# Ranking all eight experts of a mixture layer at its entry, with four instead of five taken at three passes

## The chip, the cores and the metric

The kernel is one program on one core of a Trainium2 chip. The metric is device time in microseconds for one execution. Five engines of the core share its on-chip memory (SBUF): TensorE (matmuls, into PSUM), VectorE, ScalarE, GpSimd and SyncE. Here SyncE only issues DMA. They synchronise by semaphores.

## The reference

Two decoder layers on 256 tokens of width 1024, in float32. Each has a mixer (gMLP beside latent attention) and a channel part; the second layer's channel part is a mixture of eight experts, two for each token. What matters here, cut short:

```python
logits = xt @ w_router + b_router                      # 256 tokens, 8 experts
top_val, top_idx = lax.top_k(logits, 2)
gates = softmax(top_val)
# every expert e, on the tokens that chose it:
hb = silu(xb @ w1[e]) * (xb @ w3[e])                   # 1024 -> 3584
yb = hb @ w2[e]                                        # 3584 -> 1024
out[token] += gate * yb
```

## The kernel before

**Products.** To keep float32 accuracy, each weight chunk `w` is split into `hi` (rounded, ScalarE, `moe_hi`, L744) and `lo = w - hi` (VectorE, `moe_lo`, L1289), activations likewise. A product is then three matmuls (`three`, L1987 to L1989): hi*hi, lo*hi and hi*lo. For an expert with at most 64 tokens the high and low parts of the activations stand side by side as 128 stationary columns, and two matmuls do (`two`, L2475 and L2476). Such an item is "small", with 64 slots; the others are "large", with 128.

**Items and units.** The expert stage runs eight items, one for each expert. An item is seven units (`NG`); a unit covers 512 of the 3584 hidden columns and loads six chunks of 1 MB: two each of w1, w3 and w2. There are 56 units and 336 loads, always the same. `LARGE = 5` says that items 0 to 4 are large; `SMALL_AT` says at which places of the sequence the small units stand: before, `LLLLLLLSLSLSLSLLSLSLSLSLLSLSLSLSLLSLSLSLSLLSLSLSLSLLSLLL`. Item 0 is always expert 0 and comes first; experts 1 to 7 are ranked by their counts (`expert_ranks`, `expert_order`, in the slots `TABLES` after units 0 and 1), so that the largest are items 1 to 4. An expert with more tokens than its item has slots gets a spare item of 42 more loads, at the end.

**Order.** Each engine's order is written out by hand in a function `unit(n)`. TensorE does w1 of unit n, turns the hidden rows of unit n-1 (L2515, L2512), w3 of unit n, then w2 of unit n-1. So the chunks come as w1, w3 of unit n, w2 of unit n-1, and the first load of unit n is number 6n-2 (loads count from 0). ScalarE copies or applies silu to the w1 result (L1087 small, L1089 large); this marks that w1 of a unit is done. VectorE makes the product with w3 (L1814, L1823) and the low part of the hidden rows (L1818, L1827).

**Weights.** SyncE issues the loads in order (`moe_load`, L533) into a ring of seven slots (five of `raw`, two in `r6`, shown as `r`). A slot is free when VectorE has taken the residual of its last content. The expert's number is read from SBUF by `value_load` (L550) when the unit's item starts.

**Tokens of an item.** For items after the first, VectorE picks the item's columns (`select`), TensorE and VectorE make row indices (`slot_rows`, `rows`), GpSimd gathers the rows by an indirect DMA (L695), TensorE turns them (L2461), ScalarE and VectorE split them. `PREP_AT` gives the four units in which this is done. Finished items are added to memory by indirect DMA from GpSimd (L705; a large item in one, a small one in two halves). Item 0's tokens are gathered by matmuls (`gather_first`, L2400) with one-hot columns made in `first_slots`, right after the router (`top_two`, `count`, L2395). `keep_busy` (L2056) issues matmuls whose result isn't used.

## Time and profile before

| | us |
|---|---|
| median of 3 runs | 1452.86 (1452.02 to 1453.07) |
| profiled execution, device time | 1452.38 |
| its span, first to last instruction | 1450.6 |
| first product of the expert stage | 555.84 |
| last matmul issued, end | 1438.4 |

The expert stage is thus about 880 of 1450 us. The page says how long each engine was busy; matmuls overlap each other, so that a busy TensorE isn't one at its fastest. "PEclk" is the granted clock in tenths of full speed. A line of a group ends with the idle time before its instructions and who ended it.

### The profile page before, as it was taken

Reading aid. Unit: us, or ns where it says so; the run is one execution under the profiler, and the core shown is the slowest. Engines: PE = TensorE matmul, PEld = TensorE weight load, DVE = VectorE, ACT = ScalarE, POOL = GpSimd, SP = SyncE. Lnnn points to the kernel's source line nnn. Section 1 sums busy time; section 2 is a strip of 40 time slices with the busy share of each in tenths; the row PEclk is TensorE's granted clock in tenths of the full one; section 3 lists DMA queues with packets and bytes.
Section 4 is the critical chain, followed back from the end, with each engine's and each line's share of the span. In section 5 each row is a group of like instructions: output and inputs, shape, how many; then the busy total and the mean of one; then the engine's idle time right before and its main releaser. Section 6 shows DMA issues by size and latency. Waiting matters only on the chain.

```text
span 1450.6 us, 19280 instructions
## 1 busy us (share of the span) xinstructions
PE 1423.5 (98%) x7352; PEld 1204.1 (83%) x7352; DVE 1279.9 (88%) x1263; ACT 1023.5 (71%) x992; POOL 75.3 (5%) x109
## 2 busy tenths in 40 slices
PE   9999999999999999999999999999999999999996
PEld 5799889878889988888888878888888778888884
DVE  6899888977777768999999999999999999999995
ACT  2764454444577358778887888888879888988874
POOL 5000000000000000000000001000000110000000
PEclk9999999999999999999999999999999999999999
DMA  9849849987553757999999999999999999999993
GB/s 373 330 176 349 327 174 386 391 336 277 184 198 140 285 200 277 382 414 360 407 422 421 420 416 407 410 421 420 422 421 408 414 416 420 419 408 421 418 384 129
DMA packets 74278, 506.91 MB, mean 349 GB/s; under 512 B 8386, under 2 KB 8514, under 8 KB 16707
## 3 DMA queue, kind: packets, MB, share of 16 engines
q1 hardware_dynamic: 69986, 490.91, 84.2%
q0 software_dynamic: 4192, 14.70, 3.3%
q8 instruction: 60, 0.98, 0.3%
q14 instruction: 40, 0.32, 0.1%
HBM read 498.74 MB, written 6.83 MB: 349 GB/s over the span
## 4 chain that ended last, share of the span: by engine, by line
PE 55%; issue 21%; DMA 10%; DVE 10%; ACT 3%; POOL 1%; SPq 0%; DVEq 0%; ACTq 0%; POOLq 0%
PE ps L1987 15%; PE ps L1989 14%; PE ps L1988 14%; DVE lo L1289 6%; DMA raw<-in_moe_w_dram 6%; DMA r<-in_moe_w_dram 3%; PE ps L2475 2%; PE ps L2476 2%; ACT hi L744 2%; PE ps L2048 2%; PE ps L2512 1%; DMA raw<-in_w_first_dram 1%; DMA gate_m<-rows_x,gather_row 1%; PE ps L2212 1%; PE ps L2195 1%
## 5 line engine op out<-in xcount | busy, mean ns | idle before, releaser
L1289 DVE TENSOR_TENSOR lo<-raw,hi 128x2048 fp32r<-128x2048 f32 x245 | 553.4, 2286 | 24.8 <-ACT hi L744 24.2
L744 ACT ACTIVATE hi<-raw 128x2048 fp32r<-128x2048 f32 x245 | 465.2, 1920 | 53.7 <-DMA raw<-in_moe_w_dram 44.0
L1987 PE MATMUL ps<-hi,hT_hi 128*128 128x512 f32 (+3 forms) x896 | 347.9, 388 | 4.0 <-DVE hT_lo L1315 1.9
L1989 PE MATMUL ps<-hi,hT_lo 128*128 128x512 f32 (+3 forms) x896 | 342.6, 382 | 0.0
L1988 PE MATMUL ps<-lo,hT_hi 128*128 128x512 f32 (+3 forms) x896 | 342.1, 382 | 0.0
L1289 DVE TENSOR_TENSOR lo<-r,hi 128x2048 fp32r<-128x2048 f32 x91 | 206.8, 2287 | 11.3 <-ACT hi L744 10.9
L1261 DVE TENSOR_TENSOR lo<-raw,hi 128x2048 fp32r<-128x2048 f32 (+3 forms) x83 | 177.0, 2145 | 37.7 <-ACT hi L728 29.6
L1987 PEld LDWEIGHTS ps<-hi,hT_hi 128*128 128x128 f32 x896 | 168.3, 188 | 38.9 <-issue 5.5
L1989 PEld LDWEIGHTS ps<-hi,hT_lo 128*128 128x128 f32 x896 | 168.2, 188 | 32.0
L1988 PEld LDWEIGHTS ps<-lo,hT_hi 128*128 128x128 f32 x896 | 168.4, 188 | 29.7
L744 ACT ACTIVATE hi<-r 128x2048 fp32r<-128x2048 f32 x91 | 173.4, 1921 | 19.6 <-DMA r<-in_moe_w_dram 15.5
L728 ACT ACTIVATE hi<-raw 128x2048 fp32r<-128x2048 f32 (+3 forms) x83 | 148.0, 1798 | 47.3 <-DMA raw<-in_w_fg_dram 26.2
L1987 PE MATMUL ps<-hi,bT_hi 128*128 128x512 f32 (+1 forms) x408 | 159.9, 392 | 4.2 <-DVE bT_lo L1818 4.0
L1989 PE MATMUL ps<-hi,bT_lo 128*128 128x512 f32 (+1 forms) x408 | 157.7, 386 | 0.0
L1988 PE MATMUL ps<-lo,bT_hi 128*128 128x512 f32 (+1 forms) x408 | 157.6, 386 | 0.0
L2475 PE MATMUL ps<-hi,bT_hi 128*128 128x512 f32 x392 | 154.3, 394 | 1.7 <-issue 1.0
L2476 PE MATMUL ps<-lo,bT_hi 128*128 128x512 f32 x392 | 152.8, 390 | 0.0
L1987 PEld LDWEIGHTS ps<-hi,bT_hi 128*128 128x128 f32 x408 | 76.6, 188 | 25.8 <-DVE bT_lo L1818 6.9
L1200 DVE SCALAR_TENSOR_TENSOR raw<-raw,c_rows 128x1024 f32<-128x1024 f32 x80 | 94.5, 1219 | 0.0
L1989 PEld LDWEIGHTS ps<-hi,bT_lo 128*128 128x128 f32 x408 | 76.6, 188 | 15.2
L2475 PEld LDWEIGHTS ps<-hi,bT_hi 128*128 128x128 f32 x392 | 73.6, 188 | 18.3 <-issue 1.5
L1988 PEld LDWEIGHTS ps<-lo,bT_hi 128*128 128x128 f32 x408 | 76.6, 188 | 14.3
(352 smaller groups left out, 1774.8 us busy)
## 6 DMA issues: line engine op xcount, KB each, us to landing
raw<-in_moe_w_dram SPq DMA_DIRECT2D x245, 1024.0 KB, 11.9
r<-in_moe_w_dram SPq DMA_DIRECT2D x91, 1024.0 KB, 12.1
raw<-in_w_ada_dram SPq DMA_DIRECT2D x40, 1024.0 KB, 6.8
raw<-in_w_fd_dram SPq DMA_DIRECT2D x11, 1024.0 KB, 6.9
raw<-in_w_ga_dram SPq DMA_DIRECT2D x8, 1024.0 KB, 6.4
raw<-in_w_gb_dram SPq DMA_DIRECT2D x8, 1024.0 KB, 5.4
raw<-in_w_ab_dram SPq DMA_DIRECT2D x8, 1024.0 KB, 4.8
raw<-in_w_o_dram SPq DMA_DIRECT2D x8, 1024.0 KB, 5.7
```

Of the source, the lines that this page charges most:

```text
L728: act.activation(high_of(s, e), raw_of(r, e), ACT.Copy).then_inc(hi_done, 1)
L744: act.activation(high_of(s), raw_of(r), ACT.Copy).then_inc(hi_done, 1)
L1200: m = dve.scalar_tensor_tensor(w, w, 1.0, cbc[:, :], ALU.mult, ALU.mult, accum_out=av[:, k:k + 1])
L1261: dve.tensor_tensor(low_of(s, e), raw_of(r, e), high_of(s, e).bitcast(f32), ALU.subtract).then_inc(raw_done, 1)
L1289: dve.tensor_tensor(low_of(s), raw_of(r), high_of(s).bitcast(f32), ALU.subtract).then_inc(raw_done, 1)
L1987: pe.matmul(o, wh, mh, start=first, stop=False)
L1988: pe.matmul(o, wh, ml, start=False, stop=False)
L1989: return pe.matmul(o, wl, mh, start=False, stop=last)
L2048: m = pe.matmul(ps[:, banks[t], 0:width], h0[:, k, t * P:(t + 1) * P], w[:, at:at + width], start=(k == 0), stop=(k == K - 1))
L2195: m = pe.matmul(ps[:, S_BANK[u], n * keys:(n + 1) * keys], qT[:, h, t * P:(t + 1) * P], kT[:, h, 0:keys], start=True, stop=True)
L2475: pe.matmul(o, both, mh, start=first, stop=False)
L2476: return pe.matmul(o, both, ml, start=False, stop=last)
```

## The change

`LARGE` becomes 4, and the sequence of units `LLLLSLSLSLSSLSLSLSSLSLSLSSLSLSLSSLSLSLSSLSLSLSSLSLSLSLLL`, with new places for the preparation of items. All eight experts are ranked by their counts before the stage: `expert_order` (with the ranking in it) follows the second `first_slots`, and the one-hot columns of item 0 are made behind it, in `item_slots`, from the ranked table. SyncE reads item 0's expert too, so that every load of the stage waits for `experts_ready`. ScalarE's `moe_hi(0, 1)` and `moe_hi(2)` and VectorE's `moe_lo(0, 1)` move from the routing to the first splits of item 0's tokens. The gates and their item tables are made once before unit 0. TensorE counts the totals right after the second tile's counts, and does ten and four `keep_busy` where it did one and two. `rows(0)` and `slot_rows(0)` move from unit 1 to unit 0.

```diff
-LARGE = 5
+LARGE = 4
-SMALL_AT = [7 + 9 * k // 4 for k in range((EXPERTS - LARGE) * NG)]
+SMALL_AT = [4 + (7 * k + 3) // 4 for k in range((EXPERTS - LARGE) * NG)]
-PREPS = (0, 5, 1, 2, 6, 3, 7, 4)
+PREPS = (0, 4, 1, 5, 2, 6, 7, 3)
-PREP_AT = {5: (2, 3, 4, 5), 1: (3, 4, 6, 7), 2: (14, 15, 16, 17), 6: (17, 18, 19, 20), 3: (25, 26, 28, 29),
-           7: (31, 32, 34, 35), 4: (39, 40, 42, 43)}
+PREP_AT = {4: (0, 1, 2, 3), 1: (6, 7, 9, 10), 5: (11, 12, 14, 15), 2: (19, 20, 22, 23), 6: (23, 24, 26, 27),
+           7: (35, 36, 38, 39), 3: (39, 40, 41, 42)}
@@ SyncE
-                if g == 0 and i:
+                if g == 0:
                     sp.wait_ge(experts_ready, 1)
                     expert[i] = sp.value_load(info[0:1, i:i + 1], min_val=0, max_val=EXPERTS - 1)
@@ ScalarE
             upto("m1.wo3")
-            moe_hi(0, 1)
...
             m.then_inc(xn_ready, 1)
-            moe_hi(2)
...
                 for b in (2 * h, 2 * h + 1):
                     first_high(b)
+                moe_hi(h)
+            moe_hi(2)
@@ VectorE
-            moe_lo(0, 1)
...
+            def expert_order():
+
+                dve.wait_ge(count_full, T + 1)
+                dve.tensor_copy(cnt, ps[:, R_BANK[1], 32:32 + E]).then_inc(ov_ready, 1)
+                dve.wait_ge(ov_ready, 1)
+                other = cnt.unsqueeze(1).to_broadcast([P, E, E])
+                own = cnt.unsqueeze(2).to_broadcast([P, E, E])
+                dve.tensor_tensor(cmp[:, 0], other, own, ALU.is_gt)
+                link(dve.tensor_tensor(eq[:, 0], other, own, ALU.is_equal))
+                link(dve.tensor_tensor(eq[:, 0], eq[:, 0], lt_mask[:, :, :], ALU.mult))
+                link(dve.tensor_tensor(cmp[:, 0], cmp[:, 0], eq[:, 0], ALU.add))
+                link(dve.reduce_sum(order, cmp[:, 0], AX))
+                link(dve.tensor_tensor(perm, order.unsqueeze(1).to_broadcast([P, E, E]),
+                                       eidx[:, :].unsqueeze(2).to_broadcast([P, E, E]), ALU.is_equal))
+                link(dve.tensor_tensor(ee, perm, eidx[:, :].unsqueeze(1).to_broadcast([P, E, E]), ALU.mult))
+                link(dve.reduce_sum(info_f[:, 0:E], ee, AX))
+                dve.tensor_copy(info[:, 0:E], info_f[:, 0:E]).then_inc(experts_ready, 1)
+                dve.wait_ge(experts_ready, 1)
...
             first_slots(1)
+            expert_order()
+            item_slots()
...
-                    first_low(h)
-                first_low(2)
-                first_low(3)
+                    first_low(2 * h)
+                    first_low(2 * h + 1)
+                    moe_lo(h)
                 moe_lo(2)
-                counted()
-                link(dve.tensor_copy(pg[:, :], slot_x[:, :, 0]))
+                gates()
+                item_gates()
+                picked(0, 0)
@@ TensorE
+            pe.wait_ge(sel_ready, 2)
+            count(0, 40, [(ones, 0), (before, 1)])
+            count(R_BANK[1], 32, [(ones, 0), (ones, 1)])
+            keep_busy(10, X_BANK[1])
             pe.wait_ge(hot0_ready, 1)
             gather_first(0, 0)
...
```

## Rows read from the trace of the kernel before

**Rows 1.** The page: busy time of the engines, and DMA in 40 slices.
```profile
PE 1423.5 (98%) x7352; PEld 1204.1 (83%) x7352; DVE 1279.9 (88%) x1263; ACT 1023.5 (71%) x992; POOL 75.3 (5%) x109
...
DMA  9849849987553757999999999999999999999993
```

**Rows 2.** Table by stretches: each engine's busy us, granted clock, DMA share, GB/s.
```profile
576.00:692.00 116.00, 115.41 (x535) 95.42 (x534) 110.27 (x112) 91.33 (x78) 4.90 (x3) 1.00 0.98 385
700.00:800.00 100.00, 99.95 (x474) 83.33 (x473) 97.19 (x60) 83.49 (x60) 0.00 (x0) 1.00 1.01 422
800.00:1350.00 550.00, 542.96 (x2568) 449.96 (x2567) 519.94 (x333) 467.15 (x372) 32.68 (x12) 1.00 1.01 416
```

**Rows 3.** Instructions in order of time, ScalarE: copies behind w1, units 2 and 3.
```profile
593.27 0.58 ACT L1089 ACTIVATE r<-ps 128x512 f32<-128x512 f32 x1
...
610.06 0.58 ACT L1089 ACTIVATE r<-ps 128x512 f32<-128x512 f32 x1
```

**Rows 4.** Instructions in order of time, TensorE: start, duration; first product, then pitch.
```profile
555.84 0.54 PE L1987 MATMUL ps<-hi,hT_hi 128*128 128x512 f32 x1
...
559.42 0.39 PE L1987 MATMUL ps<-hi,hT_hi 128*128 128x512 f32 x1
559.64 0.39 PE L1988 MATMUL ps<-lo,hT_hi 128*128 128x512 f32 x1
...
691.39 1.89 PE L2512 MATMUL ps<-r 128*128 128x64 f32 x16
```

**Rows 5.** Who waited for whom, 700 to 1400 us: total, times, longest.
```profile
ACT hi L744 <- DMA raw<-in_moe_w_dram: 41.1, 67, 2.0
```

**Rows 6.** Loads of line 533 from 700.2 to 1344.8 us: duration, first and last start.
```profile
L533 SPq DMA_DIRECT2D raw<-in_moe_w_dram x180: 332/333/337, 700.3 to 1344.7; - x180
...
L533 SPq DMA_DIRECT2D r<-in_moe_w_dram x72: 332/333/336, 705.2 to 1335.0; - x72
...
DMA to landing us min/median/max: 7.8/12.3/14.7
```

**Rows 7.** Three loads issued from 554.5 to 555.4 us into an empty queue.
```profile
DMA to landing us min/median/max: 4.8/8.4/10.4
```

**Rows 8.** Groups of instructions: busy us, mean ns, idle before and releaser.
```profile
L1289 DVE TENSOR_TENSOR lo<-raw,hi 128x2048 fp32r<-128x2048 f32 x245 | 553.4, 2286 | 24.8 <-ACT hi L744 24.2
L744 ACT ACTIVATE hi<-raw 128x2048 fp32r<-128x2048 f32 x245 | 465.2, 1920 | 53.7 <-DMA raw<-in_moe_w_dram 44.0
...
L1814 DVE TENSOR_TENSOR r<-r,ps 128x512 f32<-128x512 f32 x35 | 23.9, 682 | 1.9 <-PE ps L1989 1.6
```

**Rows 9.** Instructions in order of time, SyncE: first loads (merged; first start, time, count).
```profile
506.07 24.35 SPq L533 DMA_DIRECT2D raw<-in_moe_w_dram  x5
530.46 24.41 SPq L533 DMA_DIRECT2D r<-in_moe_w_dram  x2
```

**Rows 10.** Instructions in order of time: VectorE, second tile's slots, and two steps of the ranking.
```profile
552.17 0.17 DVE L1621 SCALAR_TENSOR_TENSOR r<-ps,r 128x8 f32<-128x8 f32 x1 [0.78 <-PE ps L2395]
...
570.50 0.22 DVE L1677 TENSOR_TENSOR r<-r 128x64 f32<-128x64 f32 x1
570.75 0.23 DVE L1678 TENSOR_TENSOR r<-r,lt_mask 128x64 f32<-128x64 f32 x1
```

**Rows 11.** Line 550, SyncE's reading of an expert's number: ns min/median/max.
```profile
L550 SPq TENSOR_LOAD <-info x7: 263/267/475, 644.3 to 1251.4; - x7
```

**Rows 12.** TensorE's wait for the first gather; all seven gathers' landing.
```profile
PE ps L2461 <- DMA gate_m<-rows_x,gather_row: 0.9, 1, 0.9
...
DMA to landing us min/median/max: 9.8/10.4/11.6
```

**Rows 13.** Load 311, issued at 1347.2, and the copy behind unit 52's w1.
```profile
DMA to landing us min/median/max: 12.1/12.1/12.1
...
1372.23 0.58 ACT L1087 ACTIVATE r<-ps 128x512 f32<-128x512 f32 x1
```

**Rows 14.** Table by stretches, the end of the program.
```profile
1440.00:1451.00 11.00, 0.00 (x0) 0.00 (x0) 4.50 (x8) 0.23 (x2) 0.00 (x0) 0.66 0.28 101
```

## What the change will do to the time: the prediction

> **What bounds the kernel now.** I read the page first, then a table by stretches, then who waits for whom, then single units. The page puts TensorE at 98%, VectorE at 88%, and the sixteen DMA engines at nearly 9 tenths from the 20th slice on [rows 1]. That leaves two candidates, so the expert stage is cut into stretches [rows 2]. From 576 to 692 us (seven units of item 0, all three passes) DMA brings 385 GB/s. From 700 to 800, with no indirect DMA, it brings 422; from 800 to 1350 it brings 416. The clock is 1.00, full speed, in all of them. The copies of ScalarE behind each w1 say what sets the first stretch: the large units 2 and 3 follow each other at 16.8 us [rows 3], more than six loads at the full rate need, for a load is 1.0486 MB, so 422 GB/s is 2.49 us a load, 14.9 us a unit.
>
> TensorE's own need per unit comes from its pitch: 0.23 us (559.42 to 559.64) from one 512-column matmul to the next, although each is shown as 0.39 long [rows 4]. Three passes are 72 of them, 16.4 us, plus the transposes, which with its waits is the 17 us seen. Two passes are 48, 10.9 us, and 16 short ones with 1.9: about 12.6. So the seven-unit opening is TensorE's, and after 700 the mean of TensorE (five of the one and four of the other, about 15.0) and DMA are within a few tenths. Who waits decides: from 700 to 1400 ScalarE waits 41.1 us, in 67 places, for weights to land in the five slots of `raw` alone [rows 5]. And 252 loads issued from 700.3 to 1344.7 took 12.3 us to land, against 4.8 for one issued into an empty queue [rows 6, 7]: about three others lie before each. A stream with a queue in front of it is what ends last. VectorE is close behind: six residuals of 2.29 us and two operations of 0.68 for the hidden part are 15.1 a large unit [rows 8]; they overlap by a few hundredths each, and the change leaves this as it is but for 0.5 us in seven units.
>
> The Trainium skill ("Perfetto Trace Analysis", Identifying the Most-Contended Engine) says that the busy share of TensorE doesn't tell how near it is to its limit. The trace agrees: 99.95 of 100 us are "busy" in a stretch where the pitch leaves room.
>
> **The change, part by part.**
>
> *Passes.* One item goes from three passes to two: seven units lose 24 matmuls each and gain twelve or so short ones, 17.0 - 12.6 = 4.4 us, 31 us of TensorE in all. The weights loaded remain 336. While DMA sets the pace this is worth nothing by itself. It shortens two things: how long the opening holds DMA below full rate (four three-pass units in a row instead of seven), and how far TensorE is behind the newest weights.
>
> *Does it fit?* I routed the reference's own inputs: the counts per expert are 18, 44, 16, 98, 107, 73, 31, 125. Ranked, the fifth has 44, under 64, and the first 125, under 128, so no spare item appears.
>
> *The head start is lost.* Item 0 was expert 0, so six of its loads were issued by 530.8 and three more at 554.5 to 555.4, before the routing was used [rows 9]. Now the first load waits for the ranking. The chain: the second tile's slots are computed at 552.17. The totals' count is one more pair of matmuls on two tiles, estimated at 0.4 like its neighbour, so the copy of counts starts at 552.6. Behind it come nine small operations of the ranking, which exist now too and follow each other at 0.25 us (570.50 to 570.75), the first two closer [rows 10]. So the cast ends at 554.9. SyncE reads the number in up to 0.48 us [rows 11]; with the address work behind it I take 0.9 to the issue (bounds 0.5 and 2): first load at **555.9**. Seven loads can then go at once, and the first lands after 4.9, at 560.8.
>
> *What the opening loses besides.* Copy and residual (1.92 + 2.29 [rows 8]) put TensorE's first product at about 565, against 555.84 now [rows 4]; the gathering matmuls that now follow the ranking end near 561, before that, so they cost nothing; with that cover gone they would cost a microsecond or two. The first w1 is done at 571, against 561.7. The gates and item tables (about 3.4 us of VectorE between residuals) move from the table slots of units 0 to 2 to ahead of unit 0's fourth residual; what is queued behind is every residual, and TensorE waits. That puts unit 1 at 585, unit 2 at 602, unit 3 at 619, at TensorE's 17 us. The stream's own line (560.8 + 2.49 for each load) is 573, 588 and 603 for these units' weights, so TensorE is 12 to 16 us behind a landing, where in the present opening the whole chain was over 20 behind and loads were held back.
>
> *Gather of the first small item.* Its rows are chosen in unit 1 and turned in unit 2. Now a gather lands 10.4 us after its issue, and TensorE waited 0.9 for the first [rows 12]. In the new place the index is ready near 594 and TensorE comes at 603, two or three microseconds before the rows. It costs TensorE that, in a stretch where it has less to give.
>
> *Early loss of the stream.* Put together, 0 (nothing held back) to 13 us (57 loads to unit 11 at the 385 GB/s pace of rows 2, 2.72 instead of 2.49 us). I take 1.5: the lag stays below the present opening's.
>
> *The stream.* The 252 loads of rows 6 are 251 intervals in 644.4 us, 2.567 each; at 2.49 they would be 625.0, so 19.4 us went to five gathers and seven scatters between them. Weighing a gather or a half scatter of 64 rows 1 and a whole accumulating scatter 2, that is 15 parts of 1.3 us. The new schedule has, before load 311, seven gathers, three whole and six half scatters: 19 parts, 24.7 us.
>
> *Sum.* Load 311 is the last that unit 52 needs for its gate product (the same number in both orders, and units 52 to 55 are small, large, large, large in both; 51 is large in both).
> 555.9 + 4.9 = 560.8; + 311 x 2.49 = 774.4, 1335.2; + 24.7 = 1359.9; the engines of a long queue don't end together (the third of three, issued 0.9 behind the first, lands after 10.4, where 4.8 + 2 x 2.49 - 0.9 would be 8.9 [rows 7]), 1.5 to 4, taken 2.5: 1362.4; + early loss 1.5: 1363.9. Now the load lands at 1347.2 + 12.1 = 1359.3 and its unit's copy is at 1372.23, 12.9 later [rows 13], where bare copy, residual and eight matmuls are 6.0: TensorE is behind. After the change it has 4 small in 7 units, 14.5 us a unit, against 15.4 of the stream; I take 10 (bounds 7 and 13). Copy of unit 52 at 1373.9, 1.7 later than now. The tail (three large units at TensorE's pace, drain, output) is unchanged, 78.4 us: span **1452.3**. Around the span lie 1452.38 - 1450.6 = 1.8, giving 1454.1; the profiled run is 0.5 below the median of the timed ones, so **1454.6**.
>
> **The rivals.**
>
> *A, the forecast, head start and shorter lag cancel:* 1450.5 to 1457.5. For it: every term is a row, and the sum lands 2 us from the present.
>
> *B, TensorE was the bound after all:* then 31 us less, plus the 9 us of the late start: about 1431. For it stands the 98% of the page; against it 422 GB/s with three loads queued.
>
> *C, the lag goes to its floor and nothing is lost early:* 7 instead of 10 and 0 instead of 1.5: 1450.1, at the edge of faster; with the 1.5 of spread, 1449.
>
> *D, slower: the opening fills the ring.* The place is units 1 to 10; the mechanism is late gates on VectorE, the early gather, and four 17 us units on top, so that loads wait for free slots. It decides from the point where a unit's first load is issued 29 us or more before its copy, as now in units 2 to 6. Price: half to all of the 13 us: 1459 to 1466, say 1462.
>
> *E, slower: TensorE's clock.* The granted clock reads 0.66 in the last stretch, after the last matmul at 1438.4, and 1.00 everywhere before, so here it fell to its half level only after a pause longer than any in the routing [rows 14]. The new opening has pauses of about 3 us (561.8 to 565, then between halves of w1), each broken by 1 to 3 us of matmuls. If it fell there, 7 us at half speed cost 3.5 in the opening, 1457.6. The Trainium skill ("TensorE: Matmul & The Clock Gate", HAM oscillation) warns against just this, products separated by waits for weights; no row of before shows a fall in such a pause.
>
> *F, it doesn't do what it says* (a spare item runs): 42 loads at 2.49, 105 us more, 1559. The counts exclude it but for a near tie.
>
> **How the numbers follow.** A 0.52, B 0.04, C 0.08, D 0.27, E 0.08, F 0.01. The forecast is A's 1454.6. Leaving out B, the far halves of C and D, and F leaves 1449.5 to 1462. A change of 0.2% (2.9 us) is about what can be told from none: the same means 1450.0 to 1455.8. Faster: B, most of C: 0.11. Slower: D, most of E, the upper end of A: 0.38. Same: 0.51.
>
> **What would show it.** First load near 555.9 and first product near 565; loads at 2.49 from there and 422 GB/s already before 692 (were it 385, D); copies of two-pass pairs within 13 us of a landing; the clock at 1.00 around 560 to 580; unit 52's copy near 1374 and 78.4 us behind it. Wrong would be the sum's first term if SyncE takes longer to read the expert, its third if the pace of loads depends on more than the queue, and the whole of it if the rate in the middle rises when TensorE has room, which is B.

## The result, and the profile after

| | before | after |
|---|---|---|
| median | 1452.44 us (4 runs, 1451.95 to 1453.07) | 1463.62 us (4 runs, 1461.62 to 1465.47) |
| profiled execution, device time | 1452.38 | 1465.47 |
| its span | 1450.6 | 1463.7 |
| copy behind w1 of units 0, 1, 2, 3 | 561.7, 575.9, 593.3, 610.1 | 575.8, 594.1, 611.3, 630.1 |
| of units 7, 14, 52 | 677.7, 782.5, 1372.2 | 689.7, 797.5, 1385.1 |

The changed kernel takes 1.0076 times as long, 95% interval 1.0059 to 1.0094, which is 11.2 us more. The forecast was 1454.6, with a range up to 1462.0. The page of the changed kernel (busy time; granted clock, DMA share and GB/s in 40 slices):

```profile
PE 1410.8 (96%) x7290; PEld 1193.4 (82%) x7290; DVE 1275.7 (87%) x1262; ACT 1026.3 (70%) x1006; POOL 80.3 (5%) x110
...
PEclk9999999999999998999999999999999999999998
DMA  9849849986544608999999999999999999999993
GB/s 374 325 178 346 331 174 393 379 353 243 200 173 166 252 30 343 376 376 422 417 398 421 421 409 420 421 421 407 409 421 421 420 422 408 408 420 420 416 389 129
```

TensorE is busy 12.7 us less than in [rows 1], and the time went up. (The split alone takes off 22.8, from the 1433.6 of the first experiment below; the new opening, with more fillers and a lower clock, puts 10 back. The prediction had 31 for the split.) The 16th slice (549 to 585 us) moves 343 GB/s, the 15th only 30: nothing runs ahead of the stage any more, and in the 16th the clock (PEclk) shows 8 tenths. The table by stretches, to be read beside [rows 2] (busy us of TensorE, its weight loads, VectorE, ScalarE, GpSimd; granted clock, DMA share, GB/s):

```profile
576.00:692.00 116.00, 112.79 (x522) 93.31 (x523) 107.15 (x96) 89.13 (x72) 2.30 (x1) 0.99 0.98 393
700.00:800.00 100.00, 96.72 (x468) 79.89 (x467) 97.02 (x66) 85.29 (x76) 6.33 (x2) 1.00 1.01 411
800.00:1350.00 550.00, 527.49 (x2508) 437.12 (x2507) 517.08 (x330) 469.45 (x376) 29.68 (x12) 0.99 1.01 417
554.00:560.00 6.00, 6.00 (x25) 5.02 (x25) 3.53 (x18) 0.22 (x1) 0.00 (x0) 0.72 0.46 158
566.00:572.00 6.00, 4.61 (x12) 3.31 (x12) 4.17 (x6) 4.14 (x4) 0.00 (x0) 0.72 1.01 427
```

The middle moves as much as before (417 against 416 GB/s) with 15 us less of TensorE in 550. The delay is largest at unit 3, 20.0 us; units 4 to 7 give 8.0 back, and from there to unit 52 it moves between 10 and 16, with no trend. The opening, in order of time. VectorE: the ranking's cast, then what it does until its second and third residual.

```profile
555.47 0.17 DVE L1637 CAST info<-r 128x8 int32<-128x8 f32 x1
...
561.15 0.73 DVE L1858 TENSOR_SCALAR r<-ps,scale_shift 128x128 f32<-128x128 f32 x2 [3.21 <-PE ps L2400]
...
564.89 2.29 DVE L1289 TENSOR_TENSOR lo<-raw,hi 128x2048 fp32r<-128x2048 f32 x1 [1.77 <-ACT hi L744]
...
570.42 4.49 DVE L1289 TENSOR_TENSOR lo<-raw,hi 128x2048 fp32r<-128x2048 f32 x2 [1.35 <-ACT hi L744]
```

TensorE in the same stretch: the count, ten fillers (each is shown as two records), the gathering products, the first product (it was at 555.84 [rows 4]).

```profile
552.16 0.39 PE L2395 MATMUL ps<-r,ones 128*128 128x8 f32 x2 [1.93 <-DVE r L1613]
...
553.08 6.25 PE L2056 MATMUL ps<-mask,ident 128*128 128x256 f32 x20
559.16 3.73 PE L2400 MATMUL ps<-r,x_tok 128*128 128x128 f32 x32
...
567.24 0.51 PE L1987 MATMUL ps<-hi,hT_hi 128*128 128x512 f32 x1 [2.62 <-DVE lo L1289]
```

The engines hand one chain to each other: ranking, gathering products (behind fillers that run partly at half clock), scaling, first copy, first residual. VectorE idles 3.2, 1.8 and 1.4 us in it. SyncE's first seven loads and their landing, where [rows 9] had the first at 506.07:

```profile
556.61 2.66 SPq L533 DMA_DIRECT2D raw<-in_moe_w_dram  x5
559.45 1.26 SPq L533 DMA_DIRECT2D r<-in_moe_w_dram  x2
```

```profile
DMA to landing us min/median/max: 6.3/12.3/17.9
```

Late in the stage: ScalarE's waits for weights from 700 to 1400 us (the row beside [rows 5]), the landing of load 311, issued at 1360.3, and unit 52's copy (beside [rows 13]):

```profile
ACT hi L744 <- DMA raw<-in_moe_w_dram: 36.6, 64, 2.5
```

```profile
DMA to landing us min/median/max: 11.5/11.5/11.5
```

```profile
1385.09 0.59 ACT L1085 ACTIVATE r<-ps 128x512 f32<-128x512 f32 x1
```

### The profile page after: what moved, and what is told of

Its sections match the earlier page's. It is cut to its first block, busy times and chain, and to the rows that moved or that the text cites. A ratio compares the mean times of both kernels' runs of the same rounds, so it can differ in the third digit from the quotient of the medians.

```text
span 1463.7 us, 19227 instructions
## 1 busy us (share of the span) xinstructions
PE 1410.8 (96%) x7290; PEld 1193.4 (82%) x7290; DVE 1275.7 (87%) x1262; ACT 1026.3 (70%) x1006; POOL 80.3 (5%) x110
## 4 chain that ended last, share of the span: by engine, by line
PE 68%; issue 15%; DVE 8%; DMA 5%; ACT 2%; POOL 0%; SPq 0%; DVEq 0%; ACTq 0%; POOLq 0%
PE ps L1987 16%; PE ps L1989 16%; PE ps L1988 16%; PE ps L2475 5%; PE ps L2476 5%; DVE lo L1289 4%; PE ps L2048 2%; DMA r<-in_moe_w_dram 2%; PE ps L2512 2%; DMA rows_y<-gate_m,scatter_row 1%; ACT hi L744 1%; PE ps L2212 1%; PE ps L2195 1%; DMA gate_m<-rows_x,gather_row 1%; DMA c_rows<-rows_x,gather_row 1%
## 5 line engine op out<-in xcount | busy, mean ns | idle before, releaser
L1289 DVE TENSOR_TENSOR lo<-raw,hi 128x2048 fp32r<-128x2048 f32 x245 | 553.2, 2287 | 26.7 <-ACT hi L744 26.1
L1987 PE MATMUL ps<-hi,hT_hi 128*128 128x512 f32 (+3 forms) x784 | 305.2, 389 | 7.5 <-DVE lo L1289 3.9
L1989 PE MATMUL ps<-hi,hT_lo 128*128 128x512 f32 (+3 forms) x784 | 300.1, 383 | 0.0
L1988 PE MATMUL ps<-lo,hT_hi 128*128 128x512 f32 (+3 forms) x784 | 299.9, 382 | 0.0
L1289 DVE TENSOR_TENSOR lo<-r,hi 128x2048 fp32r<-128x2048 f32 x91 | 206.8, 2287 | 7.9 <-ACT hi L744 7.7
L2475 PE MATMUL ps<-hi,bT_hi 128*128 128x512 f32 x448 | 178.6, 399 | 17.4 <-DVE bT_hi L1829 11.9
L2476 PE MATMUL ps<-lo,bT_hi 128*128 128x512 f32 x448 | 176.4, 394 | 0.0
L1987 PE MATMUL ps<-hi,bT_hi 128*128 128x512 f32 (+1 forms) x352 | 137.8, 392 | 4.5 <-DVE bT_lo L1820 4.5
L1989 PE MATMUL ps<-hi,bT_lo 128*128 128x512 f32 (+1 forms) x352 | 135.8, 386 | 0.0
L2475 PEld LDWEIGHTS ps<-hi,bT_hi 128*128 128x128 f32 x448 | 85.2, 190 | 38.8 <-DVE bT_hi L1829 14.0
L2475 PE MATMUL ps<-hi,bT_lo 128*128 128x512 f32 x224 | 89.1, 398 | 0.9 <-DVE lo L1289 0.8
L2476 PE MATMUL ps<-lo,bT_lo 128*128 128x512 f32 x224 | 87.5, 391 | 0.0
```

The source lines that it names most:

```text
L1289: dve.tensor_tensor(low_of(s), raw_of(r), high_of(s).bitcast(f32), ALU.subtract).then_inc(raw_done, 1)
L1987: pe.matmul(o, wh, mh, start=first, stop=False)
L1988: pe.matmul(o, wh, ml, start=False, stop=False)
L1989: return pe.matmul(o, wl, mh, start=False, stop=last)
L2475: pe.matmul(o, both, mh, start=first, stop=False)
L2476: return pe.matmul(o, both, ml, start=False, stop=last)
```

## The experiments

At the outset stands theory 1: the late opening is all of the loss, and removed passes pay only where TensorE sets the pace. Its rivals: a removed pass counts everywhere (2), the clock falls of the opening are the loss (3), or the serial order is, whatever the loads do (4). Ratios are to the kernel before, on the same chip, with their 95% interval. The experiments ran on several chips, on which the kernel before took 1452.0 to 1453.4 us, so a difference between two experiments is good to 1 us at best.

### Is it the opening or the split? Four combinations

**e1_entry_five**: the new opening, five large items in the old sequence.

```diff
-LARGE = 4
+LARGE = 5
-SMALL_AT = [4 + (7 * k + 3) // 4 for k in range((EXPERTS - LARGE) * NG)]
+SMALL_AT = [7 + 9 * k // 4 for k in range((EXPERTS - LARGE) * NG)]
...
```

> The opening of the changed kernel (first load waits for the ranking, all eight experts ranked at once) with the old split of the items: five of 128 slots with three passes, three of 64 slots, in the old sequence of units. Theory 1, the late opening is the whole loss and the removed passes pay only where TensorE sets the pace (units 4 to 7, where the delay shrank from 20 to 12 us): the 8 us that were given back are gone, 1463.6 + 8 = about 1471, and unit 14 comes 20 us later than before the change. Theory 2, the removed passes are worth their TensorE time everywhere (busy 20 us more with five large items): about 1484. If the split is worth nothing at all: 1463 to 1465.

Measured 1469.18 us, 1.0115 (1.0098 to 1.0132), near the 1471 of theory 1: unit 7 is 16.5 us late against 12.0 in the change. It is 1.8 less than expected, and the traces show why: here unit 3 came at 626.7, 16.6 late, and not 20.0. The changed kernel prepares its first small item in units 0 to 3, and its unit 3 lies 18.8 us behind unit 2, where this one has 16.8; of that TensorE waits 1.29 for the gather. So 3.4 of the 20.0 us come with the new split and not with the new opening, and the 8.0 that the split gives back are 4.5 net.

**e2_head_four**: four large items, with the first item's loads and first conversions where they had been.

```diff
-                if g == 0:
+                if i == 0 and g == 0:
+                    expert[0] = 7
+                elif g == 0:
                     sp.wait_ge(experts_ready, 1)
...
             upto("m1.wo3")
+            moe_hi(0, 1)
...
+            moe_hi(2)
...
-                moe_hi(h)
-            moe_hi(2)
...
+            moe_lo(0, 1)
...
-                    moe_lo(h)
```

> The new split (four and four) with the old head start: the first item's expert is written into the kernel as a constant (it is expert 7 for these inputs), so its loads and its first conversions stand where they stood before the change; all other items still wait for the ranking. Theory 1 (the loss is the head start): unit 0's copy is back at 562 to 565, the passes still return 8 us in units 4 to 7, and the time is 1452.4 - 8 = 1444, range 1443 to 1450. Theory 4 (the loss is the serial order of the ranking and selection work in the opening, whatever the loads do): 1458 to 1463. If transfers alone set the pace from the first load on: 1452.

Measured 1454.15 us, 1.0011 (1.0001 to 1.0020): neither the 1444 of theory 1 nor the 1458 of theory 4, and 2 us above the 1452 of a stream that alone sets the pace. The first copy came at 571.1, not 562 to 565.

**e3_loads_early**: as e2, but only the change on SyncE.

> The changed kernel with only the first item's loads early (its expert a constant); its conversions stay where the change put them, behind the ranking. If the loss is in the transfers (8 transfers less in the ring when the experts begin): the first copy may stay at 575, but the units behind it come 5 to 8 us earlier, 1456 to 1459. If the loss is the chain from the ranking to the first product (conversions, gather, one-hot, products at half clock): the first copy stays at 574 to 576, unit 1 at 592 to 594, and the time 1462 to 1464.

Measured 1464.07 us, 1.0086 (1.0069 to 1.0103), not to be told from the changed kernel, by the medians. Its four times spread over 6.5 us; in its profiled execution, the fastest of the four, the units came some 3 us earlier than in the change (unit 3 at 626.9), so a small gain of the early loads isn't excluded.

**e4_clock**: fillers in the pauses.

```diff
+            keep_busy(6, X_BANK[1])
             pe.wait_ge(sel_ready, 2)
...
-            keep_busy(4, X_BANK[1])
+            keep_busy(14, X_BANK[1])
```

> The changed kernel with 16 more filler products in the opening's pauses of TensorE (6 ahead of the count, 10 behind the gather), so that the clock does not fall to half at about 554, 568 and 578 us. Rival (the three falls of 3.4 us each at half clock are the loss, 1.7 us each): 1458 to 1459. Theory 1 (TensorE mostly waits for VectorE's and ScalarE's conversions there): 1462 to 1464, with the first copy less than 2 us earlier.

Measured 1462.38 us, 1.0065 (1.0048 to 1.0082). Two of the three falls are gone, and the third is hardly shorter (0.80, where the changed kernel has 0.73 from 578 to 584 us):

```profile
554.00:560.00 6.00, 6.00 (x43) 5.64 (x42) 3.82 (x18) 1.26 (x4) 0.00 (x0) 1.00 0.46 160
566.00:572.00 6.00, 4.82 (x22) 3.68 (x21) 4.43 (x4) 5.98 (x6) 0.00 (x0) 1.00 1.00 421
578.00:584.00 6.00, 6.00 (x23) 4.83 (x22) 3.09 (x4) 4.45 (x3) 0.00 (x0) 0.80 1.02 423
```

The first copy comes 2.0 us earlier, and the time is down by 1.2 us, within both intervals. Theory 3 falls as the main cause as far as the first two falls go; the third, some 3 us at half clock by the 0.73, was not removed.

**e8_old_opening_four**: the kernel before, with expert 7 pinned as item 0 and four large items, small units from unit 6.

```diff
-LARGE = 5
+LARGE = 4
-SMALL_AT = [7 + 9 * k // 4 for k in range((EXPERTS - LARGE) * NG)]
+SMALL_AT = [6 + (17 * k + 3) // 10 for k in range((EXPERTS - LARGE) * NG)]
...
-            expert = {0: 0}
+            expert = {0: 7}
...
```

> The kernel before with its opening as it was (first item known beforehand, its gather, one-hot and loads not behind the ranking) and four large items in place of five; expert 7, which is ranked first for these inputs, is the pinned one so that the items are those of the changed kernel, and the small units begin at unit 6 as their tables come no sooner. Theory 1 (the loss is the whole opening; the passes pay only where TensorE sets the pace): unit 0's copy at 561 to 563, 4 to 8 us ahead of the kernel before by unit 14, time 1452.5 - 4 to 8 = 1445 to 1449. Rival (four large items are worth nothing once the loads run ahead, as with the first conversions restored alone): 1452 to 1454.

Measured 1451.30 us, 0.9993 (0.9984 to 1.0003): no change that can be told.

| | five large | four large |
|---|---|---|
| old opening | 1452.3 (before) | 1451.3 (e8) |
| new opening | 1469.2 (e1) | 1463.6 (the change) |

Each against the kernel before on its own chip, the opening costs 12.2 us with four large items and 16.7 with five. The split returns 5.5 us with the new opening and 1.0 with the old one. So theory 1 has the place right, and misses something in the split: where the stage starts on time, four large items gained 1.0 us and not 4 to 8. One thing isn't held fixed in this table: in e8 the first small unit is unit 6, as its tables come no sooner, in the change it is unit 4. How much of 5.5 against 1.0 is due to that, no run separates.

What separates e3 from e2 is only that three copies and two residuals (some 10 us of ScalarE and VectorE) are done while the router waits. By the medians it is worth 9.9 us, all of the 9.5 from e2 to the change; in the two profiled executions it is 5.4. The table by stretches gives each engine's work up to 586 us, VectorE's being the third pair. The kernel before, then e8, e2, e3 and the change:

```profile
506.00:552.00 46.00, 45.35 (x283) 40.22 (x282) 28.99 (x51) 28.02 (x39) 3.98 (x6) 1.00 0.45 166
552.00:586.00 34.00, 33.67 (x166) 28.11 (x166) 30.94 (x48) 28.09 (x27) 0.00 (x0) 1.00 0.94 358
```

```profile
506.00:552.00 46.00, 45.44 (x283) 40.29 (x281) 29.58 (x51) 27.38 (x38) 3.77 (x6) 1.00 0.45 160
552.00:586.00 34.00, 33.58 (x166) 28.11 (x167) 30.31 (x49) 28.00 (x28) 0.21 (x1) 1.00 0.93 350
```

```profile
506.00:552.00 46.00, 44.95 (x280) 40.02 (x278) 29.30 (x46) 26.54 (x38) 2.93 (x3) 1.00 0.45 162
552.00:586.00 34.00, 32.49 (x162) 27.55 (x163) 26.48 (x64) 20.95 (x23) 1.08 (x4) 0.95 0.71 266
```

```profile
506.00:552.00 46.00, 44.76 (x279) 39.85 (x277) 24.89 (x45) 23.12 (x36) 3.13 (x3) 1.00 0.43 161
552.00:586.00 34.00, 27.93 (x135) 22.86 (x136) 25.52 (x63) 21.98 (x22) 0.89 (x4) 0.95 0.60 217
```

```profile
506.00:552.00 46.00, 43.94 (x272) 39.01 (x270) 24.77 (x48) 23.75 (x37) 3.94 (x6) 1.00 0.06 25
552.00:586.00 34.00, 28.68 (x125) 23.39 (x126) 21.95 (x55) 20.33 (x20) 0.07 (x1) 0.85 0.91 374
```

Up to 586 us VectorE has done 59.9, 59.9, 55.8, 50.4 and 46.7 us of work. Against e8 that is 0, 4.1, 9.5 and 13.2 us short for e8, e2, e3 and the change; the spans of these same executions are 0, 3.4, 8.8 and 13.4 us longer. Bytes don't order them: the change moved 374 GB/s there and e3 217, and neither wins. The match is weaker than it looks. e3's profiled execution was the fastest of its four and the change's the slowest; their medians are equal, though 3.7 us of VectorE's work lie between them. And an engine that waits for a late chain has done less by 586 us whatever sets the pace. The rows suggest theory 5 and don't show it: what the opening loses is VectorE's time, and TensorE's or the transfers' only in places. The next runs test it.

### Is it VectorE? The first item at two passes

**e9_small_first**: the old opening, expert 0 first and known beforehand, as an item of 64 slots; the other seven are ranked, four of them large.

```diff
-SMALL_AT = [7 + 9 * k // 4 for k in range((EXPERTS - LARGE) * NG)]
+SMALL_AT = list(range(NG)) + [7 + 9 * k // 4 for k in range(3 * NG)]
...
-            expert = {0: 0}
+            expert = {4: 0}
...
-                link(dve.tensor_scalar(orank[:, 0:1], orank[:, 0:1], 4.0 * SEQ, None, ALU.add))
+                link(dve.tensor_scalar(orank[:, 0:1], orank[:, 0:1], -4.0 * SEQ, None, ALU.add))
...
```

> The old opening with expert 0 still first and known beforehand, but as an item of 64 slots with two passes (it has 18 tokens for these inputs); the other seven are ranked, four of them large. Units 0 to 6 lose the third pass; from unit 7 on the sequence of large and small is that of the kernel before. Theory 1 (units 1 to 6 ran at TensorE's 17.2 us each before, and would run at the transfers' 15.0 to 15.4): 6 units x 1.8 to 2.2 = 11 to 13 us earlier by unit 7, nothing later, time 1440 to 1443. Rival (transfers and conversions set the pace of the opening too, which moved 385 GB/s against 416 later): 1448 to 1452.

Measured 1453.58 us, 1.0006 (0.9996 to 1.0015). Theory 1 is off by 11 us, and the time lies above the rival's 1448 to 1452 too: units 0 to 7 still took 16.4 us each (559.8 to 674.3) with TensorE free for 15 of 106 us (row below).

**e10_small_half_residual**: e9, with VectorE's residual made for half the columns of loads 4 to 69 (units 1 to 11). It leaves out the low parts of the other half.

```diff
+                    e = 1024 if 4 <= c < 70 else CH
-                    dve.tensor_tensor(low_of(s), raw_of(r), high_of(s).bitcast(f32), ALU.subtract).then_inc(raw_done, 1)
+                    dve.tensor_tensor(low_of(s, e), raw_of(r, e), high_of(s, e).bitcast(f32), ALU.subtract).then_inc(raw_done, 1)
```

> The kernel with expert 0 first as an item of 64 slots (e9), and VectorE's residual made for half the columns of transfers 4 to 69, units 1 to 11 (the low halves are then wrong; the order stays). Theory 5 (the opening of e9 ran at VectorE's pace: 2.29 us a residual, 13.7 us a unit, with 1 to 2 us of hidden layers and the tables beside it, and the transfers wait for the buffers that VectorE frees): units 1 to 7 take 15.0 instead of 16.4 us, and the time falls by 7 to 10 us, to 1443 to 1446. Rival (the transfers themselves ran slower there, 387 GB/s at a busy share of 0.99): 1451 to 1454.

Measured 1442.51 us, 0.9931 (0.9914 to 0.9947): 11 us below e9, and a little below what was expected. Rows of e9, then of e10:

```profile
586.00:692.00 106.00, 91.10 (x437) 74.50 (x437) 98.34 (x106) 87.50 (x84) 4.76 (x3) 0.95 0.99 388
```

```profile
586.00:692.00 106.00, 100.34 (x496) 84.08 (x495) 66.91 (x112) 97.67 (x92) 6.66 (x4) 0.97 1.01 416
```

The rival was the DMA share: 0.99 in e9, which reads like a full queue. With 31 us of VectorE's work gone the same engines move 416 GB/s instead of 388: in e9 VectorE sets the pace. A load is only issued when VectorE has taken the residual of its slot's last content, but the size of that wait can't tell who sets the pace. SyncE's queue from 586 to 692 us, in the change and in e10:

```profile
SPq L533 <- DVE lo L1289: 90.2, 40, 5.3
```

```profile
SPq L533 <- DVE lo L1290: 88.6, 44, 4.0
```

With a ring that is full it waits for a slot in either case, at 391 GB/s as at 416. Only taking work off the engine shows it.

The Trainium skill ("VectorE: DVE Perf Modes", The perf-mode tier table) gives a float32 tensor_tensor of 2048 elements 2293 ns, with no faster mode; the rows show 2287, so the trace agrees. Six in each unit are 13.7 us by the rows, and 13.8 by that page's figure, as an estimate.

**e12_small_tables_late**: e9 with four table steps moved.

```diff
-            TABLES = {0: expert_ranks, 1: expert_order, 2: item_tables, 4: overflow, 5: spare_ranks, 6: spare_experts, 7: spare_tables}
+            TABLES = {0: expert_ranks, 1: expert_order, 2: item_tables, 20: overflow, 21: spare_ranks, 23: spare_experts, 24: spare_tables}
```

> e9 (expert 0 first with 64 slots) with the four steps of VectorE that prepare the spare items (some 20 small operations) moved from units 4 to 7 to units 20 to 24. Theory 5: the 4 us of VectorE that they take come off the opening, and as the middle is set by the transfers they cost nothing there: 1449 to 1451. If VectorE did not set the pace of units 4 to 7: 1452 to 1454.

Measured 1449.20 us, 0.9981 (0.9972 to 0.9991), some 4 below e9, as theory 5 had it. It beats both kernels, by 2.8 and some 14 us. For the given inputs the pinned expert's 18 tokens fit its 64 slots; with more than 64 a spare item would run.

### The middle

**e5_two_passes**, **e6_half_residual** and **e7_half_loads** are the changed kernel with one of three resources relieved in units 12 to 51: TensorE, which leaves out the third pass of w1 and w3 in large units; VectorE, which leaves out half of each residual; and the transfers, which leave out half of each load.

```diff
+                        elif 12 <= n <= 51:
+                            pe.matmul(ps[:, bank, :], xh[:, k, :], wh[:, w], start=k == 0, stop=False)
+                            m = pe.matmul(ps[:, bank, :], xh[:, k, :], wl[:, w], start=False, stop=k == K - 1)
```

```diff
+                    e = 1024 if 70 <= c < 308 else CH
```

```diff
+                if 70 <= r - NR < 308:
+                    sp.dma_start(raw_of(r, 1024), src[:, 0:1024]).then_inc(raw_full[RING[r][0]], 16)
```

> The changed kernel with the third pass (low of x by high of w) left out of w1 and w3 in the large units 12 to 51: 16 products of 0.213 us less in each of 18 units, 61 us of TensorE less in the middle (accuracy is lower, the rest is computed). If the transfers set the pace of the middle, as the half residual has it: 1461 to 1464. If a pass still counts in a large unit there: 1440 or less.

> The changed kernel with VectorE's residual made for only half the columns of transfers 70 to 307 (units 12 to 51), 238 x about 0.96 us = 228 us of VectorE work less; the low halves are then wrong, which changes nothing of the order. If the transfers alone set the pace of the middle: 1461 to 1464. If VectorE's chain (slot freed late, landing to copy 16 us) holds the transfers back: down to about 1450.

> The changed kernel with transfers 70 to 307 at half their size (the other half of each weight tile is left stale), 238 x 1.24 = about 295 us of transfer time less. If the transfers set the pace of units 12 to 51, the units fall from 15.1 us to what VectorE and TensorE need (VectorE busy 94%, TensorE 94% of the middle: 14.2 us each): 40 units x 0.9 = 36 us less, about 1428. If VectorE or the ring of buffers already sets the pace: 1458 to 1463.

Measured 1464.10 us, 1.0086 (1.0069 to 1.0103); 1462.85, 1.0068 (1.0052 to 1.0085); 1450.63, 0.9985 (0.9976 to 0.9995). The rows from 780 to 1350 us of the change, e5, e6 and e7:

```profile
780.00:1350.00 570.00, 547.49 (x2608) 454.02 (x2607) 536.29 (x340) 486.81 (x393) 29.68 (x12) 0.99 1.01 417
```

```profile
780.00:1350.00 570.00, 512.17 (x2349) 413.43 (x2348) 537.19 (x341) 487.56 (x393) 34.89 (x12) 0.97 1.01 417
```

```profile
780.00:1350.00 570.00, 552.13 (x2624) 456.22 (x2623) 313.80 (x340) 487.78 (x393) 16.50 (x12) 0.99 1.01 417
```

```profile
780.00:1350.00 570.00, 560.11 (x2679) 466.50 (x2678) 549.83 (x348) 491.05 (x403) 31.06 (x12) 1.00 0.68 221
```

TensorE may lose 35 us, or VectorE 222, and the bytes stay at 417 GB/s: the transfers set the middle. With the transfers nearly halved only 13 us come off, not 36, and VectorE is at 550 of 570 and TensorE at 560: one of the two stands right behind them, and e7 doesn't tell which. The sums are as close: a large and a small unit together cost VectorE 12 x 2.287 + 2 x 0.684 + 2 x 0.420 = 29.65 us, TensorE 17.0 + 12.6 = 29.6 by the prediction's figures, and 12 loads at 2.49 are 29.9; units 51 to 53 came at 15.4 and 14.3, 29.7.

### Does the same hold in the two kernels compared?

**e11_after_half_residual**: the changed kernel with e10's edit.

> The changed kernel with the same halved residual in transfers 4 to 69 (low halves wrong, order the same). Theory 5: units 1 to 3 fall to TensorE's 17.0 us from 18.1 and the first product's wait for lo shortens, 3 to 6 us less, 1457 to 1460. If TensorE and the ranking alone hold the opening: 1462 to 1464.

Measured 1460.37 us, 1.0058 (1.0041 to 1.0075), 3.3 less than the change; the intervals overlap, the four times of each don't. Its row beside the change's, where TensorE is busy 104.21 and VectorE 100.24 of the same 106 us at 391 GB/s:

```profile
586.00:692.00 106.00, 106.00 (x503) 88.59 (x502) 63.78 (x88) 83.89 (x68) 2.72 (x2) 1.00 0.99 405
```

With VectorE relieved by 36 us TensorE has no pause left: four large units in a row are TensorE's, 17.2 us each. Theory 5 thus explains e9 and only some 3 us of the 11 in the changed kernel.

**e14_before_tables_late**, **e15_old_opening_four_late** and **e13_after_tables_late** move the table steps of e12 (here to units 20, 21, 22 and 24) in the kernel before, in e8 and in the changed kernel.

> The kernel before with the same four steps moved to units 20 to 24. Units 4 to 6 are large and TensorE is busy for all of them (17.2 us each): if TensorE sets their pace, 1451.5 to 1452.5, no change. If VectorE does: 1448 to 1449.

> The old opening with four large items (e8) with the same four steps moved. Small units begin at 6, so units 4 and 5 are TensorE's at 17.3 us and from 6 on VectorE's: theory 5 gives 1 to 3 us less than e8's 1451.3, 1448 to 1450. If the transfers set it: 1451 to 1452.

> The changed kernel with VectorE's four steps for the spare items moved from units 4 to 7 to units 20 to 24. Units 4 to 7 alternate small and large there, so TensorE has room: if VectorE sets their pace (theory 5), 3 to 4 us less, 1459 to 1461. If the transfers or the late start alone set it: 1463 to 1464.

Measured 1451.41, 0.9994 (0.9984 to 1.0003); 1449.39, 0.9984 (0.9974 to 0.9993); 1465.97, 1.0090 (1.0073 to 1.0107). In the kernel before, units 4 to 7 are TensorE's and nothing is gained; in e8 1.9 us are. e13 went the other way by 2.3 us, against theory 5 (the intervals of e13 and the change overlap). Its trace has a longer wait for the first gather (a row each of the change and e13, then e13's clock):

```profile
610.29 0.65 PE L2461 MATMUL ps<-ident,gate_m 128*128 128x128 f32 x4 [1.29 <-DMA gate_m<-rows_x,gather_row]
```

```profile
612.37 0.66 PE L2461 MATMUL ps<-ident,gate_m 128*128 128x128 f32 x4 [2.77 <-DMA gate_m<-rows_x,gather_row]
```

```profile
608.00:620.00 12.00, 9.23 (x39) 7.32 (x38) 8.28 (x5) 8.20 (x10) 0.00 (x0) 0.86 1.01 424
```

Behind 2.77 us of pause the clock went to its half level, 1.2 GHz, and unit 3 came 3.7 us later than in the change (0.6 of it was there from unit 0 on), in which 1.29 us left it at full. **e16_late_and_clock** and **e17_late_and_less_filler** fill that pause.

```diff
+                if n == 2:
+                    keep_busy(14, 3)
                 if n in TURN_AT:
```

> e13 (the changed kernel, spare tables moved to units 20 to 24) with 14 filler products of 256 columns in unit 2, where TensorE waits for the first gather. If the fall of the clock behind a 2.8 us pause cost e13 its gain: no half clock at 612 to 617 us, unit 3's copy back at 630, units 4 to 7 about as before, 1461 to 1463. If units 4 to 7 and the tables have nothing to do with it: 1464 to 1467, as e13.

> e13 (the changed kernel, spare tables moved late) with 5 filler products, 2.1 us at 0.43 each as the 14 of e16 took 5.99, in unit 2 where TensorE waits for the first gather. If the fall of the clock behind that pause cost e13 its gain: clock 1.00 from 608 to 620 us, unit 3's copy at 632 or earlier instead of 633.8, 1462 to 1465. If not: 1465 to 1467, as e13.

e16: 1468.89, 1.0107 (1.0090 to 1.0124); its fillers took 5.99 us, longer than the pause that they were to fill, and it says nothing on what the clock costs. e17, with `keep_busy(5, 3)`: 1464.61, 1.0087 (1.0070 to 1.0104). In its profiled execution the clock stays at 1.00 and unit 3 is at 629.8, unit 7 at 689.0, and its span is 1460.3; but its four times spread from 1462.2 to 1466.9, and their median isn't told apart from e13's. That the clock ate e13's gain is thus seen in one execution and not shown by the times. It stays open.

Copies behind w1 in the profiled executions, in us:

| | unit 0 | 1 | 7 | 14 | 52 | span |
|---|---|---|---|---|---|---|
| before | 561.7 | 575.9 | 677.7 | 782.5 | 1372.2 | 1450.6 |
| after | 575.8 | 594.1 | 689.7 | 797.5 | 1385.1 | 1463.7 |
| e1, new opening, five | 574.9 | 593.1 | 694.2 | 798.9 | 1387.9 | 1466.1 |
| e2, converted early | 571.1 | 585.9 | 681.2 | 788.9 | 1375.4 | 1453.7 |
| e3, loads early | 574.5 | 591.2 | 686.6 | 795.9 | 1380.9 | 1459.1 |
| e8, old opening, four | 562.3 | 576.6 | 676.0 | 784.2 | 1371.8 | 1450.3 |
| e9, small first | 559.8 | 576.7 | 674.3 | 782.2 | 1373.9 | 1452.1 |
| e10, half residual | 561.3 | 579.4 | 666.0 | 773.4 | 1363.0 | 1441.4 |
| e12, tables late | 560.0 | 578.3 | 673.5 | 780.0 | 1369.6 | 1447.9 |

## Why the prediction was wrong, by its own steps

**The first load**: forecast 555.9, came at 556.6, for the second tile's slots came 0.7 later than in [rows 10]; the steps behind them took what was forecast. It landed 6.3 later, not 4.9 as an empty queue had it: 562.9 against 560.8. Right in kind, 2.1 us short.

**"Copy and residual put TensorE's first product at about 565"**, first copy at 571: the product came at 567.24, which is the late landing and nothing else, and the copy at 575.8, 8.6 behind it and not 6. The step took the parts one behind another but not the order on each engine: VectorE's scaling of the second half stands behind the first residual, so the copies of chunks 1 and 2 wait for it, and the halves of w1 come apart. Of the 4.7 us that e2 gets back, e3 has 1.3 from early loads alone (574.5) and the conversions beforehand make 3.4. That e2's 571.1 is the forecast to 0.1 us is luck: the forecast was for late loads.

**Unit 1 at 585, 14 us behind unit 0**: 594.1, 18.2 behind. Gates and item tables stand ahead of unit 0's fourth residual as said; what wasn't said is that VectorE then idles 2.9 us for unit 0's w3, because its next residuals stand behind the hidden product in its order. In the kernel before that wait was 0.8.

**The early gather, two or three microseconds**: TensorE waited 1.29, but unit 3 came 18.8 us behind unit 2, where the same opening without this gather (e1) has 16.8.

**Early loss of the stream, 1.5**: this is the step that failed, by a term that was sized too small. Load 311 was issued at 1360.3 and landed 11.5 later, 1371.8, where 1363.9 was forecast. 1371.8 - 562.9 - 774.4 - 24.7 - 2.5 = 7.3 us of early loss, inside the stated bounds of 0 and 13 and far from the value taken. The rates agree: 393 GB/s from 576 to 692 us where 422 was forecast is 8.0 us lost. The reason given for the small value was that TensorE would be less far behind, so that loads aren't held back. They were held back nearly as in the kernel before (385 GB/s). By whom is shown only in part. Slots are freed by VectorE's residuals, 2.29 us each, and with half of that work gone (e11) load 311 landed at 1368.7, 3.1 us earlier, or 1.2 earlier than in e5, whose opening is the change's. The rest, 4 us or more, stays with VectorE relieved and TensorE busy for 106.00 of 106 us, which points to the four large units in a row. In e9, with TensorE free, VectorE's pace alone holds the stream at 388 GB/s. Which share each has in the changed kernel stays open.

**The lag of unit 52, 10**: it was 13.3 (1385.1 - 1371.8), against 12.9 before, outside the bounds of 7 and 13. The step let the lag shrink because TensorE needs 14.5 us a unit. VectorE needs 14.8 on the mean of a pair against the transfers' 14.9, which would forbid catching up, but that isn't the reason either, or not alone: with VectorE relieved by 222 us in the middle (e6) the lag was 11.8, with TensorE relieved (e5) 11.8, and in e3, with neither, 11.8 too. What holds it stays open.

**The tail, 78.4**: 78.6. **The side traffic and the 2.49**: 417 GB/s in the middle, as said. **Around the span**: 1.8, as said; but the profiled run lay 1.9 above the median and not 0.5 below, a matter of which of four executions was profiled. The account: 7.9 (load 311) + 3.3 (lag) + 0.2 (tail) - 2.3 = 9.1 against the missing 9.0.

**The rivals.** B (TensorE the bound) is out by e5. D had the place (the delay is largest at unit 3), the price, 1459 to 1466, which holds the result, and as far as these runs tell the mechanism: late gates on VectorE, the early gather, and four 17 us units, so that loads wait for slots. The rate from 576 to 692 us was 393, near the 385 that the prediction had given as D's sign. What it didn't have is that VectorE alone would keep the pace low if the units were shorter, as e9 shows. E happened, in part: the clock fell near 554, 567 and 578 us behind pauses that the prediction took for harmless, and e4 puts the first two falls at about 1 us, less than the 3.5 it allowed for all. (Its 1457.6 is 3.5 on the 1454.1 of the profiled run; on the forecast it is 1458.1.) C went the other way. A, at 0.52 with D at 0.27, was given too much: its two gains (lag and early loss) both rested on TensorE's room.

## What to carry to other kernels

When a chain loses its head start, count the work that was done under the old cover, for every engine, and not only as latency of the first item: two residuals and three copies done while the router waited were worth 9.9 us by the medians, and the loads alone nothing that could be told. Whether they count as an engine's time or as a longer chain, these runs don't separate. Before crediting a lighter engine with catching up, work out the floor of every other engine in the same unit; here VectorE's and the transfers' were 0.25 us apart in 30, so relieving TensorE by 35 us or VectorE by 222 gave nothing, and nearly halving the transfers gave 13 of a hoped-for 36. And neither a DMA share of 0.99 nor a load queue that waits for slots 90 of 106 us tells what sets the pace: both looked the same with VectorE relieved and the rate 7% up. Take work off one engine at a time.

## What the runs showed of the hardware that was not expected

The DMA share read 0.99 at 388 GB/s and 1.01 at 416 in the same stretch of e9 and e10: the share stayed near one while the rate still had 7% to rise.

TensorE's clock fell from 2.4 to 1.2 GHz in the opening behind pauses of 1.93 us (552.16, in a stretch where TensorE was busy 4.07 of 6 us) and of 2.77 us (e13), and not behind one of 1.29 us (unit 2). The falls near 567 and 578 us came behind 2.62 and 1.63 us. The length of the pause doesn't settle it: in e11, with the same code there, the same pause of 1.93 us and the same 4.07 of 6 us, the clock stayed at 1.00 from 554 to 560 us (0.72 in the changed kernel), and so it did in e17. The prediction had judged from rows without any fall that such pauses are harmless. In e5 the mean granted clock of the program was 0.979 and its time that of the changed kernel: where TensorE had been given room, the falls cost nothing that could be told.

Kernels with the new opening can spread more from run to run: four times of e3 lie within 6.5 us, of e13 within 5.3 and of e17 within 4.8, against 3.0 for nineteen of the kernel before beside e13. Others with it, e1, e4 and e11, lie within 2.1. What makes them spread was not tried.
